# A two-layer model in one kernel: the recurrent mixer's preparation with early parameter rows and reordered exponentials, and the input in four parts on the weights' queue

## What is computed

```python
def first_block(x, ...):
    u = x @ w_in[i]                                   # (256, 2048) @ (2048, 10544)
    u_r, u_m, u_g = _split(u, [RWKV_COLS, MLSTM_COLS, GATE_COLS])     # RWKV_COLS = 3360
    y_r = _rwkv7_mixer(u_r, mu_shift[i], w0[i], w_w2[i], ...)
...
def _rwkv7_mixer(z, mu, w0, w_w2, a0, w_a2, w_g2, k_k, k_a, r_k, lnx_w, lnx_b):
    z_prev = jnp.pad(z, ((0, 0), (1, 0), (0, 0)))[:, :-1]
    z = z + mu * (z_prev - z)
    r, k, v, zw, za, zg = _split(z, [R_WIDTH, R_WIDTH, R_WIDTH, DECAY_LORA, AAA_LORA, GATE_LORA])
    w = -jax.nn.softplus(-(w0 + jnp.tanh(zw) @ w_w2).astype(F32)) - 0.5
    decay = jnp.exp(-jnp.exp(w))
    a = jax.nn.sigmoid((a0 + za @ w_a2).astype(F32))
    g = jax.nn.sigmoid(zg) @ w_g2
    kk = k * k_k
    kk = kk / jnp.maximum(jnp.sqrt(jnp.sum(kk * kk, -1, keepdims=True)), 1e-12)
    k = k * (1.0 + (a - 1.0) * k_a)
    y = _rwkv7_scan(r, decay, k, v, kk, a)            # in chunks of 64 tokens in the kernel
    ...
    bonus = jnp.sum(r * k * r_k, -1, keepdims=True) * v
```

## Time and profile before

| | us |
|---|---|
| median of three runs | 3280.09 (3277.99 to 3285.0) |
| profiled execution | 3282.7 |
| its span, first to last instruction | 3280.7 |
| PE busy in the span | 3062.8 (93%) |
| DVE, ACT, POOL busy | 1548.6, 840.6, 263.6 |
| mean granted TensorE clock | 0.959 |

### The profile page before, as it was taken

One profiled execution on the slowest core, in us unless ns is written; L12 is line 12 of the kernel. 1 busy time (PEld: TensorE's weight loads), 2 busy tenths in 40 slices (PEclk: granted clock), 3 DMA queues, 4 the chain that ended last, 5 costly groups with the idle time before them and its releaser, 6 DMA issues.

```text
span 3280.7 us, 42679 instructions
## 1 busy us (share of the span) xinstructions
PE 3062.8 (93%) x18308; PEld 2198.1 (67%) x18308; DVE 1548.6 (47%) x1862; ACT 840.6 (26%) x928; POOL 263.6 (8%) x245
## 2 busy tenths in 40 slices
PE   8988999898999999999999999979999998999998
PEld 6777777788987753333333333368868888997886
DVE  4454544555465622222222222257987554444655
ACT  3333222433433420111011100010000343443343
POOL 2042111000000000000000000035440000000000
PEclk9998988889999899999999999989999999999899
DMA  6543221234565579999999999843334455787443
GB/s 207 157 144 104 66 72 54 84 110 151 183 220 178 191 277 424 425 425 425 425 425 425 425 425 425 374 149 116 118 120 122 139 170 126 181 190 162 95 157 139
DMA packets 214401, 722.11 MB, mean 220 GB/s; under 512 B 16122, under 2 KB 18586, under 8 KB 163644
## 3 DMA queue, kind: packets, MB, share of 16 engines
q1 hardware_dynamic: 209628, 700.12, 60.7%
q0 software_dynamic: 3216, 14.97, 1.3%
q10 hardware_dynamic: 1360, 4.19, 0.3%
HBM read 717.13 MB, written 2.10 MB: 219 GB/s over the span
## 4 chain that ended last, share of the span: by engine, by line
PE 73%; DMA 11%; DVE 10%; ACT 3%; issue 1%; POOL 1%; DVEq 0%; ACTq 0%; POOLq 0%
PE psum L137 72%; DMA t<-in_w_up 11%; DVE t L283 7%; ACT t L254 2%; DVE t L294 1%; PE psum L143 1%; ACT t L256 1%; DVE t L298 0%; POOL t L328 0%; DVE t L306 0%; POOL t L323 0%; DMA t<-in_r_k 0%; ACT L254 0%; DVE t L269 0%; DVE t L275 0%
## 5 line engine op out<-in xcount | busy, mean ns | idle before, releaser
L137 PE MATMUL psum<-t,t 128*128 128x256 f32 (+10 forms) x17230 | 2962.2, 381 | 153.4 <-DVE t L283 67.9
L137 PEld LDWEIGHTS psum<-t,t 128*128 128x128 f32 (+4 forms) x17230 | 2102.2, 177 | 976.4 <-issue 586.1
L283 DVE TENSOR_TENSOR t<-t,t 128x1024 fp32r<-128x1024 f32 (+7 forms) x642 | 782.6, 1219 | 559.1 <-ACT t L254 521.7
L254 ACT ACTIVATE t<-t 128x1024 fp32r<-128x1024 f32 (+7 forms) x521 | 528.6, 1015 | 979.8 <-PE psum L137 695.3
L283 DVE TENSOR_TENSOR t<-t,psum 128x1024 f32<-128x1024 f32 (+3 forms) x265 | 246.4, 930 | 741.6 <-PE psum L137 441.0
L254 ACT ACTIVATE t<-psum 128x1024 f32<-128x1024 f32 (+5 forms) x278 | 213.7, 769 | 1414.2 <-PE psum L137 1310.5
L328 POOL TENSOR_TENSOR t<-t,t 128x1024 f32<-128x1024 f32 (+9 forms) x125 | 208.2, 1666 | 577.4 <-DVE t L283 262.4
L283 DVE TENSOR_TENSOR t<-psum,t 128x1024 f32<-128x1024 f32 (+5 forms) x125 | 100.3, 802 | 123.4 <-PE psum L137 105.0
L143 PE MATMUL psum<-t,t 128*128 128x128 f32 (+1 forms) x566 | 90.0, 301 | 40.4 <-DVE t L294 18.2
L143 PEld LDWEIGHTS psum<-t,t 128*128 128x128 f32 (+1 forms) x566 | 69.8, 154 | 77.9 <-issue 39.7
L269 DVE COPY t<-psum 128x256 f32<-128x256 f32 (+4 forms) x82 | 47.8, 583 | 120.2 <-PE psum L143 68.9
(11 more groups left out here) (65 smaller groups left out, 237.5 us busy)
## 6 DMA issues: line engine op xcount, KB each, us to landing
t<-in_w_gate SPq DMA_DIRECT2D x128, 1024.0 KB, 17.0
t<-in_w_up SPq DMA_DIRECT2D x128, 1024.0 KB, 18.4
t<-in_w_down SPq DMA_DIRECT2D x128, 1024.0 KB, 17.1
t<-in_w_in SPq DMA_DIRECT2D x160, 512.0 KB, 3.5
t<-in_w_in_odd SPq DMA_DIRECT2D x128, 512.0 KB, 5.2
t<-in_w_in_even SPq DMA_DIRECT2D x96, 512.0 KB, 3.8
t<-in_w_out SPq DMA_DIRECT2D x32, 512.0 KB, 4.4
t<-in_w_pg SPq DMA_DIRECT2D x32, 512.0 KB, 4.1
```

Of the source, the lines that this page charges most:

```text
L137: ins = self.e.matmul(o, l, r, start=start, stop=stop, skip_group_check=True)
L254: self.put(self.e.activation(o, i, f, scale=scale), event)
L283: self.put(self.e.tensor_tensor(o, a, b, op), event)
```

## The change

Five edits. The input is loaded in four column parts by SP, each ahead of one of the first four weight pieces. PE turns part j between the first pieces of `ur0`: it waits for a part's halves only at the pieces that read it, and it waits for the constants only after the first eight pieces. ACT and DVE halve parts and pieces in an order written out to fit. The parameter rows go to other places (the later `RB`, `t_82`, and a place in `t_95`) and are loaded by POOL right after `mub`. In DVE's list `kk`, its square and the sums stand ahead of the copies of `rw.lo`, and both ("rw.dec2", c) stand ahead of the products that do not need them. ACT takes the four first exponentials in a row, then the two that wait for DVE.

```diff
-        par = room.rearrange("p (k c) -> p k c", k=3)
+        par = [RB.rearrange("p b c -> p (b c)")[:, 0:1024], RB.rearrange("p b c -> p (b c)")[:, 1024:2048],
+               at(lt_at + 1280, 1024)]
...
             pe.stage("in")
-            turn_into("in.xT", x, 2048, ("landed.x",), ("ident",))
-            pe.meet(0)
+            first = pieces_a(pe, "ur0", xT, 16, "w_in", 0, 512)
+            for j, part in enumerate(((0,), (0, 1), (1, 2), (2, 3, 3))):
+                turn_columns("in.xT", x, j, (f"landed.in{j}",), ("ident",))
+                for i in part:
+                    pe.wait_ge(("in.xTc", i))
+                    some(first, 1)
             pe.wait_ge(("consts",))
             for ci, c in enumerate(range(0, 3360, 512)):
                 n = min(512, 3360 - c)
-                proj_a(pe, f"ur{ci}", xT, 16, "w_in", c, n, ("in.xTc", 3))
+                if ci:
+                    proj_a(pe, f"ur{ci}", xT, 16, "w_in", c, n)
...
             def rwkv():
+                def pb(k):
+                    return two(par[k], 1024)
+
+                v.wait_ge(("landed.par",))
+                v.tt(kk, k_, pb(0), ALU.mult)
+                v.tt(BB, kk, kk, ALU.mult)
+                for b in range(2):
+                    v.red(sm[:, 0, b, :], hd(BB)[:, b], ALU.add, event=("rw.ksum",))
                 v.ahead_of("rw.lo")
...
                 v.mset(loraT[64:65, 0:2, :], 1.0, event=("ur.loraT",))
-
-                def pb(k):
-                    return two(par[:, k, :], 1024)
-
-                v.wait_ge(("landed.par",))
-                v.tt(kk, k_, pb(0), ALU.mult)
-                v.tt(BB, kk, kk, ALU.mult)
-                for b in range(2):
-                    v.red(sm[:, 0, b, :], hd(BB)[:, b], ALU.add, event=("rw.ksum",))
...
                 v.stt(k_, BB, 1.0, k_, ALU.add, ALU.mult)
+                for c in range(2):
+                    ps = half(v.bank("rw.dec", c))
+                    v.wait_ge(("rw.qb", c))
+                    v.stt(ps, sig_[:, :, 512 * c:512 * c + 512], CD, ps, ALU.mult, ALU.add, event=("rw.dec2", c))
                 v.tt(BB, r_, k_, ALU.mult)
...
                 v.tt(BB, aa, kk, ALU.mult, event=("rw.aa",))
-                for c in range(2):
-                    ps = half(v.bank("rw.dec", c))
-                    v.wait_ge(("rw.qb", c))
-                    v.stt(ps, sig_[:, :, 512 * c:512 * c + 512], CD, ps, ALU.mult, ALU.add, event=("rw.dec2", c))
...
             v.stage("in")
-            low_halves("in.xT", xT, 2048, "in.xTc")
-            v.meet(0)
+            for j in range(4):
+                v.split_to(2 * j + 1 if j else 0)
+                low_half("in.xT", xT, j, "in.xTc")
+                v.split_to(2 * j + 2)
...
+                a.ahead_of("rw.dec", 1)
                 for c in range(2):
                     cs = slice(512 * c, 512 * c + 512)
                     ps = half(a.bank("rw.dec", c))
-                    a.ahead_of("rw.dec", c)
                     a.wait_ge(("rw.dec", c))
                     a.activation(PB[:, :, cs], ps, ACT.Exp)
                     a.activation(QB[:, :, cs], ps, ACT.Exp, scale=-1.0, event=("rw.qb", c))
+                for c in range(2):
                     a.wait_ge(("rw.dec2", c))
-                    a.activation(RB[:, :, cs], ps, ACT.Exp, event=("rw.rb", c))
+                    a.activation(RB[:, :, 512 * c:512 * c + 512], half(a.bank("rw.dec", c)), ACT.Exp, event=("rw.rb", c))
                     a.free("rw.dec", c)
...
-            a.load(("landed.x",), [(x, I["x"][0].rearrange("(b p) d -> p b d", p=128))])
             a.stage("in")
-            high_halves("in.xT", xT, 2048)
-            a.meet(0)
+            for j in range(4):
+                a.split_to(2 * j + 2 if j else 0)
+                high_half("in.xT", xT, j)
...
-            g.meet(0)
             g.load(("landed.mu",), [(mub, along("mu_shift"))])
...
-            g.split_to(stream.first("w_a2") + 1)
-            g.wait_ge(("ur", 6))
-            g.load(("landed.par",), [(par[:, 0, :], along("k_k")), (par[:, 1, :], along("k_a")),
-                                     (par[:, 2, :], I["r_k"][0].rearrange("h n -> (h n)").partition_broadcast(128))])
+            g.load(("landed.par",), [(par[0], along("k_k")), (par[1], along("k_a")),
+                                     (par[2], I["r_k"][0].rearrange("h n -> (h n)").partition_broadcast(128))])
...
-            pieces(stream, 0, gate + 8)
+            whole = I["x"][0].rearrange("(b p) d -> p b d", p=128)
+            for j in range(4):
+                s.load((f"landed.in{j}",), [(x[:, :, 512 * j:512 * j + 512], whole[:, :, 512 * j:512 * j + 512])])
+                pieces(stream, j, j + 1)
+            pieces(stream, 4, gate + 8)
```

## The result

| | before | after |
|---|---|---|
| median, us | 3281.6 (3277.99 to 3285.0, 4 runs) | 3256.9 (3254.79 to 3261.72, 4 runs) |
| ratio | | 0.9927 (95% interval 0.9915 to 0.9940) |
| profiled execution, us | 3282.7 | 3257.01 |
| its span, us | 3280.7 | 3254.3 |
| opening ends (last of the first eight pieces) | 45.05 | 39.14 |

The change makes the kernel 24.7 us faster by the medians, 26.4 us by the two spans. At the transposes `rw.fm` the profiled execution is 25.6 us ahead (268.91 against 294.49), so nearly all of it is won in the two stretches that the change touches. Between them, from the end of the opening to r3, pass 161.11 us before and 161.14 us now: the transfer of the parameter rows costs PE nothing there.

The account below looks back on a forecast made before the run. PE, busy 93% of the span and 73% of the last chain, was taken as the bound. Opening 5.7 plus preparation 18.2 (10.9 + 3.7 + 3.6) gave 23.9 us, so 3280.1 - 23.9 = 3256.2, range 3250 to 3261 (chance 0.62).

Parts of the forecast that it names:

- Rivals 4 and 5: Preparation: clock stays low throughout, 3312 us, chance 0.02; or ACT still held, PE waiting at every piece, 3273, chance 0.05.
- The opening, 5.7 us: First eight pieces: first product at 9.7, end at 39.3 against 45.05, gain 5.7 us, bounds 2.0 and 8.4.
- The margins: Opening: halves ready a few tenths of a us before PE needs each part; fourth piece there at 13.4.
- The cause of the 3.89 us: Opening before the change: after turning x, PE waits 3.89 us more, for POOL's constants.
- The wait at r5, 10.94 us: Preparation: early parameter rows and sums ahead remove PE's whole wait of 10.94 us at r5.
- The wait at r11, 4.3 forecast: Preparation: reordering cuts PE's wait from 7.98 to 4.3 us, gain 3.7, bounds 0 and 5.6 (POOL at 2.35).
- POOL's subtractions mostly near 4.2 us: Sign in the timeline after: POOL, beside DVE, mostly takes near 4.2 us per subtraction.
- The clock, 3.6 us: Preparation: less time at the low clock, 1.8 us in each of two stretches, 3.6 in all, 0 to 7.1.
- DVE, 6 us in hand: End of the preparation: DVE, next to be late, finishes some 6 us before PE reaches rw.fm.
- rival 2: Preparation: DVE and POOL become the bound, the wait at r11 unchanged, gain 15.6, 3264.5 us; chance 0.14.
- Rival 1: Opening: pieces run slowly or wait, full loss 10.8, 3272.7 us; chance 0.03 full, 0.06 partial beyond 3261.
- That the shift goes through unchanged: Later stages, experts' included, start from PE and DVE events behind both stretches and move as a whole, keeping the 23.9 us.

Follow-up runs that it names:

- e2: The kernel before with the preparation's edits alone, none of the opening's: 3261.63 us, ratio 0.9932.
- e5: The kernel before with the reordered exponentials and DVE's two additions ahead of the products alone: 3275.74 us, one run.
- e1: The kernel before with the opening's edits alone, the preparation as before: 3275.35 us, ratio 0.9974.
- e8: The changed kernel with ACT making the high half of r11 ahead of the exponentials: 3252.5 us, ratio 0.9908.
- e11: e8 with ACT's copies of rw.g and the first half of ml.qk ahead of the high halves of r16 and r17: 3248.62 us, ratio 0.9886.
- e10: The changed kernel with unread transposes on PE, 16 ahead of the first turned part and 18 behind it: 3257.66 us, one run.
- e6: The kernel before with PE waiting for POOL's constants after the first eight pieces, not ahead of them: 3279.9 us, one run.
- e9: e6 without the meeting of all engines after the turning: 3282.37 us, one run.
- e3: The kernel before with the parameter rows in their new places, loaded right behind mu, and nothing else: 3271.78 us, one run.
- e4: e3 with kk, its square and the sums ahead of the copies of rw.lo in DVE's list: 3267.86 us, one run.
- e7: The changed kernel with the four parts of x loaded by ACT's queue in place of SP's: 3260.49 us, one run.

## Why the prediction was right

The time (3256.9 for 3256.2), the sign and the mechanism hold. That the time is off by only 0.7 us is luck: the four runs spread over 7 us, the forecast started from 3280.1 where four runs of the kernel before give 3281.6, and two errors in the preparation cancel (the wait at r11 and the clock, below). Rivals 4 and 5 wanted a low clock through the preparation or a wait at every piece; the row of 216 matmuls without a wait, at a clock of 1.00, rules out both. The terms one by one:

- **The opening, 5.7 us; 5.9 by the two profiles, about 5.2 by several.** Five kernels with the old opening (before, e2 to e5) end it at 42.07 to 45.05, mean 43.99, and four with the new one (the changed kernel, e1, e8, e11) at 38.07 to 39.26, mean 38.84. In the sum two errors of 1.3 us cancel. The first product came at 10.98, not 9.7: part 0 took 4.4 us to land and not the median 3.5 of a load in the middle of the kernel, and its turn 1.97 us. The three later turns took 1.29, 1.03 and 1.03 us, not 1.55 each. The quarter of 6.19 us that I took for a turn lies between these and the 1.97 us of the first one, so that row probably ran in part at the lower clock level. The margins held, but not for my reason: I had the fourth piece there at 13.4, and in e10 ACT still waits for it until 14.94. The slow first piece, 5.46 us, hid that in the changed kernel.
- **The cause of the 3.89 us was half read.** POOL's constants were the releaser in the row, but the meeting of the engines waited for them too, and with the whole of `x` turned first DVE's halves are done only 0.9 us ahead of them (e6, e9). The sum didn't rest on this.
- **The wait at r5, 10.94 us: gone**, by the steps as I put them. DVE's first operation took 3.52 us and its second 4.37 (4.4 taken); the sums ended 1.8 us after ACT began to wait. The early rows alone leave 4.75 us of it (e3), and the sums ahead take the rest (e4). With the clock of the stretch, below, this is the larger part of the gain.
- **The wait at r11, 4.3 forecast, 2.78 measured.** The mis-sized term is POOL's halving: I took about 4 us for it beside DVE's products, and it took 2.35. It started at 234.12, DVE's next product at 234.19, and it was that product that took 4.43. Of the two, the one that comes second pays. The bound (POOL at 2.35) was in the text, the choice wrong. The same choice failed as a sign: I expected POOL's subtractions mostly near 4.2 us, and of the eleven behind 200.28 four took 4.0 to 4.2 and seven 2.34 to 2.40. The rest of this chain was right: PE was through with r10 at 233.74 and the high half of r11 was ready 0.3 us later, as in the forecast (239.7 and 240.0).
- **The clock, 3.6 us; half of it is the change's.** The first 216 matmuls, without a wait in between, took 33.46 us here and 33.41 to 33.46 in e2, e4, e7 and e10, against 9.37 + 26.00 before: those 1.9 us belong to the wait that went. For the last 168 the kernels with a wait of 2.78 at r11 took 29.62, 31.10, 31.11, 31.08 and 31.11, and the kernels with the long wait 31.34, 31.68, 30.71, 30.72, 31.43 and, in e6, 27.75. So the second 1.8 us of the forecast are not borne out: the 1.7 us of the two profiles are chance, for e2, e5, e7 and e10 stand at the lower level for some 3.5 us right behind the same wait of 2.78 us, and only the changed kernel's profile does not. I had kept two thirds of that loss for `rw.pz` and the shorter wait; e8 has no wait there and still falls to 0.50 around `rw.pz`, and e6, with 27.75, is the one profile in which the clock stayed at 1.00 there. With 5.2 us at r11 where I had 3.7 and next to nothing here where I had 1.8, the sum came out right.
- **DVE, 6 us in hand; 8.5** (its products end at 260.36, PE's transposes come at 268.91), so rival 2 had no ground. Rival 1 neither: with the first piece over, no matmul of the opening was slow again (5.8 to 6.0 us for two pieces).
- **That the shift goes through unchanged** holds only within some us. Windows from `rw.fm` to the reload of `x`, in the same instructions; columns as in the earlier trace rows. Before, then the changed kernel, then e1:

```profile
294.49:953.04 658.55, 600.26 (x5966) 550.72 (x5967) 341.83 (x393) 227.28 (x284) 41.58 (x40) 0.91 0.35 108
```

```profile
268.91:930.69 661.78, 602.11 (x5966) 552.78 (x5967) 341.35 (x393) 227.30 (x284) 41.50 (x40) 0.91 0.35 107
```

```profile
289.02:941.19 652.17, 592.78 (x5966) 544.44 (x5967) 341.23 (x393) 227.15 (x284) 42.50 (x40) 0.92 0.37 109
```

The same 5966 matmuls are busy for 602.11, 600.26 and 592.78 us, and the other engines for the same time within 1 us in all three. The changed kernel lost 3.2 us of its lead here and got 4.1 back in the last stages. Windows of 5 us over these stretches tell how long the clock stood at its lower level: some 115 us before, 115 in the changed kernel, 98 in e1. In e1 17 us less at half the rate are some 8.5 us of work, and its matmuls are busy for 7.5 to 9.3 us less: there it is the clock. Between before and the changed kernel it is not, and where the 3.2 us come from is open. In the last stages (from 2144.19 before, 2121.89 in the changed kernel) it is the clock again: some 85 us at the lower level before and 74 now, with PE busy for 1086.0 and 1082.0 us. What decides how often the clock falls no run isolates. It is why one profile's span (e1: 3264.8, with a median of 3275.35) is no measure of an edit of a few us.

## What to carry to other kernels

Follow each wait of the bound engine back to the list in which some other engine is blocked, and ask what stands behind that wait without needing it. Here a half that another engine was waiting for stood behind a square root, and later behind an exponential, and moving it showed no cost in these runs. A load placed where another tensor dies comes as late as that tensor; another place for it was worth 6 us. To judge an edit of a few us, compare the stretch that it touches, over several profiles, and not the span.

## What the runs showed of the hardware

- Of a DVE product and a POOL subtraction with all operands in SBUF, the one that starts later pays for the earlier, which keeps its own time: 2.35 us for POOL and 4.43 for DVE at 234.12 and 234.19, 2.40 and 4.50 in e8, where DVE came second again; and POOL 4.21 at 236.64, behind that same product of DVE. DVE's sums (2.47) were not slowed beside POOL.
- At the very start of an execution the windows give a granted clock of 1.00 for 10 to 13 us, in which twelve matmuls of 512 columns took 5.46 us, against 3.03 after other PE work (e10). The durations tell the level there, the clock's column does not.
- The clock can fall while PE is at work: in e8 the windows give 0.50 from 239 to 245, and PE has not waited since 200.05. Behind a pause of 2.75 us sixteen transposes took 3.57 us at 0.53 (e8), behind one of 1.11 us 1.97 us at 1.00 (e11).
- Equal streams of matmuls differ by several us between executions: 27.75 to 31.68 us for the same 168, 22.55 to 24.94 us for the first 96 of the kernels with the old opening. This spread is as large as single edits of this study. For the 5966 matmuls behind them e1's 592.78 us against 600.26 go with 17 us less at the lower clock level.
- The first transfer of an execution, 512 KB, took 4.2 to 4.4 us from issue to PE's first use of it (the changed kernel, e1, e8, e11); by another queue, beside the pieces, 6.0 us (e7).
